# One-hot rows of a routed layer: compare and multiply in one VectorE operation per token, in place of two operations per four tokens

## What is computed

```python
sc = jnp.einsum('thpd,pnd->thpn', q, subkeys)          # 8 heads, 2 halves, 128 keys
top_v, top_i = lax.top_k(sc, 16)
cand_v = top_v[:, :, 0, :, None] + top_v[:, :, 1, None, :]
cand_id = top_i[:, :, 0, :, None] * 128 + top_i[:, :, 1, None, :]
best_v, best_j = lax.top_k(cand_v, 16)
ids = take_along_axis(cand_id, best_j); gates = softmax(best_v)
# per token and expert: 128 chosen out of 16384
a = einsum('td,ted->te', x, u_tab[ids])
w = gates * gelu(a)
y = einsum('te,ted->td', w, v_tab[ids])
```

## Time and profile before

| what | value |
|---|---|
| runs | 1289.13, 1291.79, 1293.04 us |
| median | 1291.79 us |
| span of the profiled execution | 1288.8 us (no other time is given for it) |
| PE, PEld busy | 1253.4 us (97%), 1136.5 us (88%) |
| DVE, ACT, POOL busy | 980.7 us (76%), 756.8 us (59%), 385.8 us (30%) |
| mean granted TensorE clock | 0.997 |
| mean DMA rate | 193 GB/s |
| rounds | from 584.2 us (first L1646) to 718.9 us (last L1632) |
| L1646, 64 operations, 128x512 | 43.8 us busy, 685 ns each |
| L1655, 64 operations, 128x512 | 43.9 us busy, 686 ns each |
| chain that ended last, by engine | PE 60%, DVE 8%, ACT 6%, issue 3%, POOL 2% |

### The profile page before, as it was taken

One profiled execution on the slowest core, in us unless ns is written; L12 is line 12 of the kernel. 1 busy time (PEld: TensorE's weight loads), 2 busy tenths in 40 slices (PEclk: granted clock), 3 DMA queues, 4 the chain that ended last, 5 costly groups with the idle time before them and its releaser, 6 DMA issues.

```text
span 1288.8 us, 26239 instructions
## 1 busy us (share of the span) xinstructions
PE 1253.4 (97%) x8596; PEld 1136.5 (88%) x8596; DVE 980.7 (76%) x1851; ACT 756.8 (59%) x1293; POOL 385.8 (30%) x254
## 2 busy tenths in 40 slices
PE   7999999999999989999999999999999999999997
PEld 7999999898999979999999888888888888888885
DVE  6999988997987767997999765656666666666666
ACT  6434454565766655558999645455555555555554
POOL 1189812225160147788888200000000000000000
PEclk9999999999999999999999999999999999999999
DMA  9978876453776245554443565556665556655662
GB/s 374 336 243 258 263 252 224 162 169 111 246 236 210 92 157 177 168 182 146 129 139 122 163 192 184 193 182 227 210 192 184 184 189 195 183 185 185 195 187 74
DMA packets 69344, 248.15 MB, mean 193 GB/s; under 512 B 7968, under 2 KB 8352, under 8 KB 68512
## 3 DMA queue, kind: packets, MB, share of 16 engines
q1 hardware_dynamic: 59920, 213.04, 51.1%
q10 hardware_dynamic: 9360, 34.27, 7.9%
HBM read 244.66 MB, written 2.62 MB: 192 GB/s over the span
## 4 chain that ended last, share of the span: by engine, by line
PE 60%; DVE 8%; ACT 6%; issue 3%; POOL 2%; DMA 0%; DVEq 0%; POOLq 0%; ACTq 0%
PE ps L2525 27%; PE ps L1952 11%; PE ps L2536 10%; PE ps L2538 5%; DVE O L1655 2%; ACT WH L506 2%; DVE O L1646 2%; PE ps L2123 1%; DVE A L1632 1%; ACT A L917 1%; DVE WL L1035 1%; ACT O2b L911 1%; POOL tmp L1891 1%; PE ps L2142 1%; ACT O2b L909 1%
## 5 line engine op out<-in xcount | busy, mean ns | idle before, releaser
L1035 DVE TENSOR_TENSOR WL<-raw,WH 128x1024 fp32r<-128x1024 f32 x320 | 407.1, 1278 | 84.4 <-ACT WH L506 81.1
L506 ACT ACTIVATE WH<-raw 128x1024 fp32r<-128x1024 f32 x392 | 409.8, 1052 | 51.8 <-PE ps L2538 19.6
L1952 PE MATMUL ps<-X,WH 128*128 128x256 f32 x1888 | 349.6, 286 | 2.0 <-DVE WL L1035 1.8
L1952 PEld LDWEIGHTS ps<-X,WH 128*128 128x128 f32 x1888 | 293.4, 192 | 3.1 <-DVE WL L1035 2.4
L1952 PE MATMUL ps<-X,WL 128*128 128x256 f32 x944 | 266.9, 283 | 0.0
L2536 PE MATMUL ps<-X,WH 128*128 128x512 f32 x576 | 205.6, 397 | 0.0
L2525 PE MATMUL ps<-WH,wvL 128*128 128x512 f32 x496 | 195.5, 394 | 0.0
L2525 PE MATMUL ps<-WL,wvH 128*128 128x512 f32 x496 | 195.3, 394 | 0.0
L2525 PE MATMUL ps<-WH,wvH 128*128 128x512 f32 x496 | 195.3, 394 | 0.0
L1918 POOL TENSOR_TENSOR WL<-raw,WH 128x1024 fp32r<-128x1024 f32 x72 | 173.5, 2412 | 59.0 <-ACT WH L506 58.9
L1952 PEld LDWEIGHTS ps<-X,WL 128*128 128x128 f32 x944 | 180.5, 191 | 0.0
(11 more groups left out here) (358 smaller groups left out, 2280.3 us busy)
## 6 DMA issues: line engine op xcount, KB each, us to landing
raw<-stream SPq DMA_DIRECT2D x392, 512.0 KB, 4.2
ada<-adaT ACTq DMA_DIRECT2D x47, 512.0 KB, 4.3
bias<-att_bias ACTq DMA_DIRECT2D x8, 512.0 KB, 4.9
x<-xT ACTq DMA_DIRECT2D x2, 512.0 KB, 5.7
raw<-stream SPq DMA_DIRECT2D x4, 256.0 KB, 5.9
ws<-wsT SPq DMA_DIRECT2D x1, 1024.0 KB, 8.4
lng<-rows SPq DMA_DIRECT2D x1, 1024.0 KB, 7.6
lnb<-rows SPq DMA_DIRECT2D x1, 1024.0 KB, 8.6
```

The source lines that it names most:

```text
L506: act.activation(WH[:, slot, :], raw[:, slot, :], ACT.Copy).then_inc(h_done, 1)
L1035: dve.tensor_tensor(WL[:, slot, :], raw[:, slot, :], WH[:, slot, :].bitcast(F32), ALU.subtract).then_inc(l_done, 1)
L1952: mm = pe.matmul(out_ap, a(kc), b(kc), start=(first and kc == 0 and i == 0), stop=(last and kc == KC - 1 and i == 2))
```

## The change

`iota` is copied once to 128 free columns of PSUM bank 3 (`iota_p`), after the wait for `lt_ready`, and DVE waits for that copy (`gate_packed` at 2). A first one-hot of one token is then one `tensor_scalar`: `iota_p` compared with the token's column of i1, the result multiplied by the token's column of the gates. Both are scalar operands, one value per partition, read from PSUM. Four of them stand where one compare of four tokens stood; `hot_gated` and `eq_ready` are gone. The wait for `gate_mm` of `hot_first` stays as it was, and `hot_ready` is given by the fourth operation of a half.

```diff
+        iota_p = ps[:, 3, T:T + NK]
...
             dve.wait_ge(lt_ready, 1)
+            dve.tensor_copy(iota_p, iota).then_inc(gate_packed, 1)
+            dve.wait_ge(gate_packed, 2)
...
                 if e >= 1:
                     dve.wait_ge(gate_mm, 2 * e - 1 + half)
-                dve.tensor_tensor(O1[:, 4 * half:4 * half + 4, :], iota4, of_four(i1_l, e, half),
-                                  ALU.is_equal).then_inc(eq_ready, 1)
-
-            def hot_gated(e, half):
-
-                o = O1[:, 4 * half:4 * half + 4, :]
-                dve.wait_ge(eq_ready, 2 * e + half + 1)
-                if e == 0:
-                    dve.wait_ge(gate_packed, 1)
-                dve.tensor_tensor(o, o, of_four(gate_l, e, half), ALU.mult).then_inc(hot_ready, 1)
+                for n in range(4 * half, 4 * half + 4):
+                    t = 8 * e + n
+                    hot = dve.tensor_scalar(O1[:, n, :], iota_p, i1_l[:, t:t + 1], gate_l[:, t:t + 1],
+                                            ALU.is_equal, ALU.mult)
+                hot.then_inc(hot_ready, 1)
 
             for e in range(ROUNDS):
                 hot_first(e, 0)
                 dve.tensor_tensor(O2a[:, :, :], iota4, of_four(i2_l, e, 0), ALU.is_equal).then_inc(hot2_ready[0], 1)
-                hot_gated(e, 0)
                 hot_first(e, 1)
                 if e >= 2:
                     product_round(e - 2)
-                hot_gated(e, 1)
                 if e >= 1:
                     gated_round(e - 1)
```

More of the change, by code:

```diff
@@ L320, in two_block_kernel @@
         hot2_ready = [sem(f"hot2_ready{i}") for i in range(2)]
-        gm_ready, prod_ready, eq_ready = sem("gm_ready"), sem("prod_ready"), sem("eq_ready")
+        gm_ready, prod_ready = sem("gm_ready"), sem("prod_ready")
         dist_ready, dist2_ready = sem("dist_ready"), sem("dist2_ready")
```

## The result

Both kernels were timed in alternation on one chip. Before: 1291.3 us, the median of 6 runs (1288.58 to 1293.04). After: **1296.95 us**, the median of 6 (1294.4 to 1297.72). The ratio is 1.0045 with a 95% interval of 1.0033 to 1.0057, so the change costs 5.8 us (4.3 to 7.4). A repetition (e7) gave 1.0043 (1.0027 to 1.0059). The profiled execution of after took 1297.22 us, 1.9 us more than its span of 1295.3; its span is 6.5 us over that of before.

The account below looks back on a forecast made before the run. DVE's work per round was taken to bound the rounds from 17 on; +0.75 (rounds 11 to 16), +3.5 (17 to 30) and -0.07 (31) gave +4.2 us, 1291.8 to 1296.0 us, range 1288.5 to 1299.5.

Parts of the forecast that it names:

- The bound: DVE's work per round sets the time from round 17 on; after the rounds TensorE is full, so changes there stay.
- The price of an operation: Each of eight 128-element DVE operations per round with two PSUM scalars: 0.33 us start to start, 0.41 long.
- the second path: Price estimate from two consecutive DVE operations with two scalars and 256 elements, all from SBUF: 0.325 us each.
- What is free: DVE's idle time ahead of early gated rounds: before round 11 a loss of up to 0.23 us costs nothing.
- The sum: Rounds 1 to 10 nothing, 11 to 16 +0.75, 17 to 30 +3.5, round 31 -0.07: together +4.2 us.
- the list of signs: Expected profile signs, among them PE's wait ahead of the second half longer by 0.25 us in late rounds.
- Moved: Product after the second half's one-hots: round length unchanged when DVE is full; round 31's last tile starts 0.32 us earlier.
- the main case: Whole kernel slower by 3 to 5 us; chance 0.62.
- Cheap: Rival: short DVE operations cost 0.25 us or less, DVE falls behind PE in late rounds, time 1287.5; chance 0.16.
- Dearer: Rival: each new DVE operation costs 0.35 us, +0.41 per round, time 1300.0; chance 0.08.
- A wait of the tile for the product: Rival: PE's next tile waits for DVE's product in the last rounds, at most some 0.1 us in a handful; no separate chance.

Follow-up runs that it names:

- e7: The after kernel run once more, unaltered, for a second profile: ratio 1.0043 to before.
- e1: The after kernel with the number row read from SBUF (`iota`) instead of its copy in PSUM, scalars still in PSUM: 1361.03 us, ratio 1.0542.
- e5: The before kernel with the change made in rounds 0 to 9 alone, copy of the number row included: ratio 0.9993.
- e9: The after kernel with the one subtraction `firstL` (round 24) moved from DVE to POOL: 1294.17 us, ratio 1.0024 to before.
- e10: The before kernel with the subtraction `firstL` moved from DVE to POOL: ratio 0.9994 to before.
- e4: The after kernel with 60 extra instructions (120 already satisfied waits) on DVE ahead of the rounds: ratio 1.0044 to before, profiled run 1293.32 us.
- e8: The after kernel with the product put back ahead of the last one-hot of the second half: 1295.33 us, ratio 1.0033 to before.
- e2: The after kernel with both scalar operands replaced by immediates (5.0 and 1.0), gates left out of the computation: 1286.32 us, ratio 0.9962 to before.
- e3: The after kernel with both scalars read from SBUF, number row still in PSUM: 1294.25 us, ratio 1.0023 to before.
- e6: The before kernel with the change made in rounds 17 to 31 alone: ratio 1.0036 to before.

## Why the prediction was right, and where it was not

**The bound: right.** The stretch after the rounds is as long as before to 0.01 us, and the loss of the rounds comes out in full.

**The price of an operation, 0.33 us: right**, 0.33 from start to start and 0.41 long (the 28 between 700 and 716 us have a median of 421 ns). Between 660 and 690 us the records are longer, 0.50 to 0.58, but four of them still take 1.32; in the repetition (e7) the same ones are 0.40 to 0.43 long. So the length of a record can change by 0.1 us and more while the cost stays. The scalars' cost is additive in a stream, as the second path had it. That this path gave the same figure was in part luck: e1 has 0.265 us for 128 elements from SBUF, 256 take 0.325 there, and only the doubled elements brought it to the 0.33 from PSUM.

**What is free: right.** DVE's idle time took up the early rounds' share (e5).

**The sum: right in size for the rounds, 3.86 us for 4.2.** From gated round to gated round in after: rounds 1 to 10 -0.12 (predicted nothing), 11 to 16 +0.53 (predicted +0.75), 17 to 31 +3.75 without what `firstL` costs (predicted 3.5 for 17 to 30 and 0.25 for 31), and -0.30 at the end, the earlier last tile (predicted -0.32). e9 less e10 gives 3.68 for rounds 17 to 31, from two profiles without the collision. PE's wait ahead of the second half grew by 0.26 and 0.27 us in rounds 29 and 30, as the list of signs had it (0.25).

**What was missed: `firstL`, +2.3 us** (130.86 less 128.53, with and without the collision, e4; e9 and e10 together give the same). Of these, 2.2 are its record and some 0.15 the granted clock behind it, which I had left out. The step that failed is the one under "Moved", that a shift inside the round changes no length when DVE is full. It holds for DVE's own sequence, but the shift also moves DVE's operations against POOL's. `firstL` had been ahead of POOL's `WL` by 0.27 us, and I didn't look at what else runs at that time. With it the sum is 0.3 + 3.9 + 2.3 = 6.5 us, the whole difference of the two spans; 0.3 of it lies ahead of the rounds, where such spans differ by up to 4.4 us in any case. The ratio of the runs gives 5.8 us, the medians differ by 5.65. That is above the main case, 3 to 5 us, and inside the range because the range was made wide for other reasons; by e9's and e10's ratios the part that the prediction had reasoned out costs 3.9.

**The rivals.** "Cheap" would have gained 4.3 us; with the scalars gone the stretch fell by 4.6, the late rounds being 3.72 to 3.81 us and not 3.85. "Dearer" is out: 0.33, not 0.35. A wait of the tile for the product cost nothing measurable (e8).

**Open.** The gated round's follower starts 0.05 us later in the late rounds of after than in before. It does so in e2 too (0.99 us, 702.42 to 703.41), so the scalars are not the cause; no run isolates what is. What spreads the runs of one kernel over 3 to 5 us stays open too. The race of `firstL` alone doesn't spread them, as e9 and e10 show, and how often it goes which way in one kernel isn't known: each profile is of one execution. Why the clock fell in after, e7 and e3 and not in e6 is open: PE was busy for 0.12 of 2 us in e3 (694 to 696 us) and for 0.14 in e6. And e4's order of records contradicts the rule by 0.12 us.

## What to carry to other kernels

When one operation over 512 elements is cut into four with scalar operands, charge each scalar (65 ns here) as well as the start of each instruction, and work out the price at which it breaks even before you build: here 0.30 us against 0.33. Before you shift an engine that is full, list the operations of DVE with two SBUF inputs that lie close to a long POOL operation: a shift of a few tenths of a microsecond can decide which of them waits. A stage bounded by the same instruction at both ends is a better yardstick than the span: it repeated to 0.1 us where the runs of before alone lie 4.5 us apart. And a collision can be worth more than its own length: look at the granted clock behind it.

## What the runs showed of the hardware

- A scalar operand per partition costs DVE 65 ns per instruction in a stream of operations on 128 fp32 elements from PSUM (0.20, 0.265, 0.33 us), whether it comes from PSUM or from SBUF (0.32).
- A DVE subtraction with two inputs in SBUF takes 0.42 to 0.50 us where its record begins before that of POOL's two-input operation (5 of 5 profiles). Where POOL's begins first it ends 0.28 or 0.29 us after POOL's (5 of 6 profiles, 1.45 to 2.63 us long; in the sixth, e4, by 0.12 us, it took 0.54 and POOL's 2.94 in place of 2.41). The profile shows no wait for that: the record is long, and no idle time stands ahead of it. It is found by comparing the duration of the same instruction between two kernels.
- A DVE `tensor_scalar` that reads its tensor from SBUF lasted up to 2.60 us beside POOL (median 0.35), where the same one from PSUM kept to 0.40 to 0.58 in after. With it the kernel is 5.4% slower, a part of which is the granted clock of 0.82 to 0.90 in the rounds.
- Sixty more instructions ahead of the rounds (e4) made no round longer than after's by 0.15 us or more.
- The granted clock fell from 1.00 to 0.50 for 3 to 4 us behind a wait of PE of 2.0 us (PE busy for 0.61 of 2 us) in after, and in e6 it did not (0.14 of 2 us).
- The records of the same DVE instructions lasted 0.50 to 0.58 us in one execution of after and 0.40 to 0.43 in another, between 660 and 690 us; four of them took 1.32 us from start to start in both.
